# Two expert matrices loaded early, a modulation row read late, and the shared expert's down products moved six experts on

## What is computed

```python
sh_m, sc_m, g_m, sh_f, sc_f, g_f = modulations(c)          # each (9, 1024)
x = x + g_m * mixer(rmsnorm(x) * (1 + sc_m) + sh_m)
xn = rmsnorm(x) * (1 + sc_f) + sh_f
# 64 experts, 8 for each token, gates normalised and scaled by 2.5
hid = silu(xn @ exp_w_gate[e]) * (xn @ exp_w_up[e])          # 1024 -> 256
routed = sum over e of (hid * gate) @ exp_w_down[e]          # 256 -> 1024
shared = (silu(xn @ shared_w_gate) * (xn @ shared_w_up)) @ shared_w_down
y = rmsnorm(x + g_f * (routed + shared))
```

## Time and profile before

| | us |
|---|---|
| median of 3 runs | 806.15 |
| lowest, highest | 804.11, 809.91 |
| the profiled execution | 808.24 |
| its span, first to last instruction | 806.5 |
| TensorE busy in it | 704.0 |
| mean granted TensorE clock | 0.964 |

### The profile page before, as it was taken

One profiled execution on the slowest core, in us unless ns is written; L12 is line 12 of the kernel. 1 busy time (PEld: TensorE's weight loads), 2 busy tenths in 40 slices (PEclk: granted clock), 3 DMA queues, 4 the chain that ended last, 5 costly groups with the idle time before them and its releaser, 6 DMA issues.

```text
span 806.5 us, 14755 instructions
## 1 busy us (share of the span) xinstructions
PE 704.0 (87%) x4965; PEld 394.9 (49%) x4966; DVE 324.4 (40%) x601; ACT 228.2 (28%) x392; POOL 301.0 (37%) x317
## 2 busy tenths in 40 slices
PE   3699999999979999999999999998789978987820
PEld 1277556445554455554555555454355534544500
DVE  3115575477335553234332332434323434242217
ACT  4212622023123232223322322323222323232202
POOL 0321021021305454456544653636445454455220
PEclk9799999999989999999999999999999999999975
DMA  8999979729559999999999999999999999999943
GB/s 324 362 305 321 336 265 322 280 80 384 190 215 396 351 396 411 359 385 383 398 385 387 393 396 398 387 407 401 404 414 403 397 399 412 400 402 403 366 104 120
DMA packets 74813, 279.08 MB, mean 346 GB/s; under 512 B 18997, under 2 KB 22193, under 8 KB 49040
## 3 DMA queue, kind: packets, MB, share of 16 engines
q1 hardware_dynamic: 51240, 252.35, 78.9%
q0 software_dynamic: 23424, 26.07, 13.7%
q10 hardware_dynamic: 104, 0.08, 0.0%
HBM read 272.54 MB, written 26.30 MB: 371 GB/s over the span
## 4 chain that ended last, share of the span: by engine, by line
PE 64%; DMA 26%; DVE 4%; issue 2%; ACT 1%; SPq 1%; POOL 0%; POOLq 0%; DVEq 0%; ACTq 0%
PE bank L1118 27%; DMA gu<-in_exp_w_up 20%; PE bank L1154 11%; PE bank L863 5%; PE bank L854 5%; PE bank L981 3%; DMA gu<-in_ada_w 3%; PE bank L1096 2%; PE bank L829 2%; PE bank L1135 1%; PE bank L866 1%; PE bank L1210 1%; DMA sh<-in_shared_w_down 1%; PE bank L1065 1%; DMA sh<-acc_rows 1%
## 5 line engine op out<-in xcount | busy, mean ns | idle before, releaser
L1118 PE MATMUL bank<-gu,et 128*64 128x256 f32 x2496 | 286.7, 384 | 34.0 <-DMA gu<-in_exp_w_up 25.0
L1118 PEld LDWEIGHTS bank<-gu,et 128*64 128x64 f32 x2496 | 183.0, 138 | 155.5 <-issue 79.5
L537 POOL DMA_INDIRECT acc_rows<-et,idx x64 | 104.6, 1635 | 241.8 <-DVE et L1642 175.4
L1154 PE MATMUL bank<-dn,et 128*64 128x512 f32 x632 | 149.8, 603 | 11.9 <-issue 9.6
L1635 DVE COPY et<-bank 128x256 f32<-128x256 f32 x64 | 27.1, 424 | 259.8 <-PE bank L1135 259.8
L725 ACT ACTIVATE et<-bank 64x512 f32<-64x512 f32 x64 | 37.8, 591 | 266.9 <-PE bank L1118 266.9
L1154 PEld LDWEIGHTS bank<-dn,et 128*64 128x64 f32 x632 | 40.4, 136 | 78.8 <-issue 78.8
L735 ACT ACTIVATE et<-bank,mb 128x512 f32<-128x512 f32 x64 | 44.0, 687 | 119.8 <-PE bank L1154 104.2
L1642 DVE TENSOR_SCALAR et<-bank,mb 128x512 f32<-128x512 f32 x64 | 48.0, 751 | 68.3 <-PE bank L1154 58.5
L1628 DVE TENSOR_TENSOR et<-et 64x512 f32<-64x512 f32 x64 | 67.9, 1061 | 0.4 <-ACT et L726 0.4
L519 POOL DMA_INDIRECT et<-xn_rows,idx x32 | 35.7, 1116 | 55.4 <-DVE idx L1617 47.9
(11 more groups left out here) (290 smaller groups left out, 630.2 us busy)
## 6 DMA issues: line engine op xcount, KB each, us to landing
dn<-in_exp_w_down SPq DMA_DIRECT2D x64, 1024.0 KB, 25.0
gu<-in_exp_w_gate SPq DMA_DIRECT2D x63, 1024.0 KB, 22.7
gu<-in_exp_w_up SPq DMA_DIRECT2D x63, 1024.0 KB, 25.1
gu<-in_ada_w SPq DMA_DIRECT2D x12, 2048.0 KB, 14.6
gu<-in_w_in SPq DMA_DIRECT2D x3, 2048.0 KB, 19.3
gu<-in_w_out SPq DMA_DIRECT2D x2, 2048.0 KB, 16.7
acc_rows<-late SPq DMA_DIRECT2D x2, 1280.0 KB, 14.8
gu<-in_w_in SPq DMA_DIRECT2D x2, 1024.0 KB, 15.3
```

Of the source, the lines that this page charges most:

```text
L537: pool.indirect_dma_start(acc_rows[u % 2], bass.IndirectOffsetOnAxis(ap=idx[:, u, 0:1], axis=0), yo[:, u % 2, 0, :], None, bounds_check=2 ...
L1118: mm = pe.matmul(bank[u % 2][64 * c:64 * c + 64, b * FE:(b + 1) * FE], xt[:, b, k % 4, k // 4, :], w[c][:, k * FE:(k + 1) * FE], start=(k ...
L1154: mm = pe.matmul(bank[5 + b][64 * c:64 * c + 64, :], hT[:, b, j, :], dn[:, dslot(u), j * D + c * HALF:j * D + (c + 1) * HALF], start=(j == ...
```

## The change

1. SP loads expert 5's gate matrix into `gmod` once the residual is done with it (`x2_done`), and expert 4's up matrix into `late` once the counting matmuls are done (`counted`). Both stand ahead of `load_gu(0, 0, 3)`. Expert 5's up matrix stays in its place in `gu`.
2. GpSimd reads `g_f` into `gmod` not before the routing but in its group 0 at u == 7, behind gather(10) and scatter(6), after a wait for expert 5's matmuls.
3. ScalarE runs `moving_tokens(0, 2)` behind xt1(1) instead of ahead of it.
4. The six halves go with experts 8 to 13 instead of 2 to 7 (`SHARED_AT = 8`), on TensorE and on VectorE. TensorE's groups 2 and 3 and VectorE's group 1 are written out instead of looped.

```diff
+SHARED_AT = 8
+        gmodf = gmod[:, :, :].rearrange("p a n -> p (a n)")
...
-                sync.dma_start(guf[sl][:, 0:KT * FE], eg[e]).then_inc(ld_gu[sl], 16)
+                if not (isinstance(g, int) and g == SLOTS + 1):
+                    sync.dma_start(guf[sl][:, 0:KT * FE], eg[e]).then_inc(ld_gu[sl], 16)
                 sync.dma_start(guf[sl][:, KT * FE:2 * KT * FE], eu[e]).then_inc(ld_gu[sl], 16)
...
             for u in range(3):
                 load_dn(0, 0, u)
+            sync.wait_ge(s["acc_zeroed"], 32)
+            sync.wait_ge(ld_shared_gu, 32)
+            sync.wait_ge(s["x2_done"], 3)
+            sync.wait_ge(ld_gu[gslot(SLOTS + 1, SLOTS + 1)], 32)
+            sync.dma_start(gmodf, eg[SLOTS + 1]).then_inc(ld_gu[gslot(SLOTS + 1, SLOTS + 1)], 16)
+            sync.wait_ge(s["counted"], 1)
+            sync.dma_start(late[:, :], eu[SLOTS]).then_inc(ld_shared_gu, 16)
             load_gu(0, 0, 3)
-            sync.wait_ge(s["acc_zeroed"], 32)
             sync.dma_start(xTf[:, 0:KT * FE], eg[SLOTS]).then_inc(ld_shared_gu, 16)
-            sync.dma_start(late[:, :], eu[SLOTS]).then_inc(ld_shared_gu, 16)
...
             pool.wait_ge(s["gf_wrote"], 64)
-            get_mods(5, gmod[:, 0, :], gmod[0:64, 1, :], "gf_in")
...
                         scatter(r, i if u else i - 1, (u - 1) % U)
+                    if first and r == 0 and u == SLOTS + 3:
+                        pool.wait_ge(s["gu_done"], SLOTS + 2)
+                        get_mods(5, gmod[:, 0, :], gmod[0:64, 1, :], "gf_in")
...
                     gates(r, i, u)
-                    if first and r == 0 and u == 0:
-                        moving_tokens(0, 2)
                     if first and r == 0 and u == 1:
                         spread_table(0)
                     if not (last and u == U - 1):
                         xt1(r, i + (u + 1) // U, (u + 1) % U)
+                    if first and r == 0 and u == 0:
+                        moving_tokens(0, 2)
...
+                if isinstance(e, int) and e == SLOTS + 1:
+                    w = (gmodf, w[1])
...
-                    half = i * V + u - 2 if r == 0 and isinstance(i, int) and 2 <= i * V + u < U else None
+                    half = i * V + u - SHARED_AT if r == 0 and isinstance(i, int) and 0 <= i * V + u - SHARED_AT < 6 else None
...
-                    now_shared = first and r == 0 and u >= U - 6
-                    if now_shared and u % 2 == 0:
-                        shared_turned((u - U + 6) // 2)
+                    half = i * U + u - SHARED_AT if r == 0 and isinstance(i, int) and 0 <= i * U + u - SHARED_AT < 6 else None
+                    if half is not None and half % 2 == 0:
+                        shared_turned(half // 2)
...
-                    if now_shared:
-                        shared_sum(u - U + 6)
+                    if half is not None:
+                        shared_sum(half)
```

More of the change, by code:

```diff
@@ L1225, in rounds @@
                 body(r, 1)
-                with pe.Fori(2, NE // V - 1) as i:
+                body(r, 2)
+                body(r, 3)
+                with pe.Fori(4, NE // V - 1) as i:
                     body(r, i)
@@ L1688, in rounds @@
                 body(r, 0, first=True)
-                with dve.Fori(1, NE // U - 1) as i:
+                body(r, 1)
+                with dve.Fori(2, NE // U - 1) as i:
                     body(r, i)
```

## The result

The changed kernel takes 812.06 us (median of 12 runs, 808.25 to 816.71), the kernel before 806.19 beside it (804.11 to 809.91). The ratio is 1.0072, with a 95% interval of 1.0050 to 1.0094: 5.9 us slower. The forecast was 802.9 with a range of 796.5 to 809.0, so its sign was wrong, its case (within 1%) right, and the range ended 3 us too low. The profiled execution of after took 811.83 us, its span is 810.1.

What follows compares the result with a forecast made beforehand. Weights end the kernel, but TensorE before about 350 us, last at expert 13's end, decides how early they come. Terms 5.2 + 1.9 - 5.7 plus 1.8 of slack gave 3.2 us: 802.9 us against 806.15, range 796.5 to 809.

Steps and rivals of the forecast that it cites:

- The method: Find how much earlier TensorE reaches expert 13's end, add the weight queue's slack there, cap by the DMA engines.
- cap: DMA engines' limit on the gain: start 5.5 us earlier plus 6.0 us from 381 rising to 403 GB/s, 11.5 in all.
- step 5: Sum at expert 13's end: 5.2 + 1.9 - 5.7 = 1.4 us ahead, plus slack 1.8: 3.2 us; cap doesn't bind.
- sign: DMA share below 1 before 350 us, not released by expert 13, would mean the method itself is wrong.
- Step 1: ScalarE's new order at expert 1: TensorE starts 3.4 us earlier, runs at 2.4 GHz; 5.2 us ahead.
- Step 2: Halves moved from experts 2 to 7 to experts 8 to 13: 1.9 us ahead at expert 13's end, nothing at the end.
- Step 3: Two matrices loaded early, into DMA gaps before 240 us: shortens nothing, price 0; at most 5 us of loss.
- Step 4: Late modulation read behind scatter 6 lands at 297.3, due 291.6: TensorE stalls 5.7 us (3.6 to 7.5) before expert 8's down matmuls.
- Rival B: Modulation read lands much later; each us beyond 15.6 of latency delays the end; at 25 us, 9.4 us slower, 815.6; 8%.
- Rival A: Modulation read lands in time, within 6.7 us of issue, so nothing stalls: 8.9 us gained, 797.3; 16%.
- C: Start at expert 1 isn't won; early lead 0 to 3.3 us, sum 2.0 us slower to 1.3 faster: 806; 14%.
- D: Before 350 us small transfers, not TensorE, limit the rate; DMA stream starts 5.5 us earlier: 800.6 if stall covered; 12%.

Runs made afterwards that it cites:

- read_u5: The changed kernel with the late modulation read two experts earlier, behind scatter 4 instead of scatter 6: 807.43 us against 807.19 for the kernel before.
- halves_10: The changed kernel with the six halves behind experts 10 to 15 instead of 8 to 13, the read unmoved: 806.86 us against 807.19 for the kernel before.
- no_gmod: The changed kernel with expert 5's gate matrix in its ring place and the modulation read before the routing: 801.93 us against 807.19 for the kernel before.
- order_only: The kernel before with ScalarE's new order alone: 801.61 us against 807.19 for the kernel before.
- tiny_read: read_u5 with the late read cut to 16 bytes from one row, modulation not the reference's: 800.81 us against 805.76 for the kernel before.
- read_act: The changed kernel with the late reads issued by ScalarE, behind its copy of expert 7's tokens: 798.90 us against 805.76 for the kernel before.
- one_read: The changed kernel with the second read from one row instead of eight, modulation not the reference's: 811.26 us against 805.76 for the kernel before.
- halves_only: The kernel before with the six halves behind experts 8 to 13 and nothing else: 805.12 us against 806.76 for the kernel before.
- order_back: The changed kernel with ScalarE's old order: 817.75 us against 806.76 for the kernel before.
- early_up_40: halves_40 with expert 4's up matrix loaded early: 797.42 us against 806.03 for the kernel before.
- halves_40: The kernel before with ScalarE's new order and the six halves behind experts 40 to 45: 796.73 us against 806.03 for the kernel before.
- halves_40_old: The kernel before with the six halves behind experts 40 to 45 and ScalarE's old order: 802.44 us against 806.03 for the kernel before.
- halves_56_old: The kernel before with the six halves behind experts 56 to 61 and ScalarE's old order: 805.50 us against 806.76 for the kernel before.
- all_56: The changed kernel with the late reads issued by ScalarE and the halves behind experts 56 to 61: 803.05 us against 806.76 for the kernel before.
- halves_56: The kernel before with ScalarE's new order and the six halves behind experts 56 to 61, nothing else: 796.74 us, ratio 0.9872 to the kernel before.

## Why the prediction was wrong

**The method held.** In the ten changed kernels where the halves come before or around expert 13 (the rows after, read_u5, halves_10, no_gmod, order_only, tiny_read, read_act, one_read, halves_only and order_back), what TensorE has won or lost at the end of expert 13 arrives at the last expert within 1.4 us, from -6.2 to +10.5. For the six with more than 10 us of lead there, it doesn't: 15.5 us ahead becomes 7.6, and 10.3 becomes 2.1. A cap exists, as step 5 had it. The forecast had named a sign that would make the method itself wrong: a DMA share below 1 before 350 us that something other than expert 13 releases. By the letter it came, 0.52 from 325 to 330 us, ended by expert 11's matmuls. The sign was badly chosen: a late TensorE lets the queue run dry earlier too, and the last dry stretch, 350 to 355, still ends behind expert 13's matmuls, which end at 350.3.

**Step 1** was right: 5.2 us forecast, 5.0 in the trace, 5.2 in order_only's change at expert 13, and 5.2 in its time (ratio 0.9936).

**Step 2** forecast 1.9 us ahead at the end of expert 13; halves_only shows 0.3. There the six halves gave back 10.6 us up to expert 8's start (experts 2 to 8 in 39.5 us instead of 50.1), and five of them took 9.8 from there to expert 13's end (60.6 instead of 50.8): a half costs 1.77 us in the old place and 1.95 in the new, and 0.8 to 0.9 is left. Expert 1's slow matmuls then took 6.40 us instead of 5.82, both behind 4.5 us of idleness; the granted clock from 232.5 to 238.9 is 0.56 there and 0.66 in before, so the edit has no part in it. That leaves 0.3.

**Step 3**, price 0, was right: with the stall taken out (tiny_read) and alone (early_up_40) the early loads change nothing.

**Step 4 failed**: the stall was forecast as 5.7 us (3.6 to 7.5) and cost 12.5. Expert 9's start to expert 10's took 20.96 us, where an expert with a half takes some 8.5. It splits in two. The idle part was 9.6. The second read was issued at 281.1, 7.7 us before the data were due (I had 6.7), but landed in 17.2 us, not in 12.4. That is the step's wrong term. I took the mean of four earlier landings of the same instruction; all four were issued before the experts' gathers and scatters shared the queue, and the row nearest in kind, the 14.2 us, was already the largest. It had busy DMA engines beside it as well (share 1.02 and 1.03 from 189 to 199 us), and its like took 14.2 to 15.2 us in the eight other traces with an early read. So of the missing 4.8 us some 2 lie in the mean, and the rest appears only where the experts' own transfers share the queue; which of them is to blame was not tried. The idle part is 17.2 less 7.7, as step 4's own rule has it. Of the other 2.9 us, 2.6 are the clock: behind the idleness the down matmuls and the half ran at 1.2 GHz. I had counted exactly this as a gain of 2.1 us in step 1 and didn't apply it to the idleness that step 4 made.

**Step 5**: the slack of 0 to 3.4 us at expert 13, taken as 1.8, wasn't there. In the changed kernel the engines run dry at 350 to 355 as soon as TensorE is late. So the sum at the end of expert 13 is 5.0 + 0.9 - 12.5 = 6.6 us behind, by the halves' and the order's measured terms; the trace shows 6.1 behind, 6.0 arrive, and the medians differ by 5.9.

The cap was mis-sized too, though it didn't bind here. I let the rate rise from 381 to 403 GB/s. In halves_40 it rises to 392 with the queue fed, worth 109 us x (1 - 381/392) = 3.1 us, and 150 us x (1 - 392/394) = 0.8 behind that. With the 5.5 us of earlier start this makes 9.4 instead of 11.5; for halves_40_old and halves_56_old it makes 3.9, and for all_56, whose stretch of 241 to 350 runs at 389 GB/s and which moves 0.75 MiB of read into it (1.9 us at 403), 5.5 + 2.2 + 0.8 - 1.9 = 6.6. These sums use rates of the kernels that they explain, so they show consistency and forecast nothing. The traces agree within 1.4 us where expert 40 begins: TensorE is 10.4, 5.3, 5.0 and 6.9 us ahead there, in the same order. That a fed stream goes no faster than 389 to 395 GB/s before 500 us is measured in six kernels; why, against 401 to 403 behind, isn't settled. The share of time is 1.02 to 1.03 in both.

The rest of the shortfall is the halves themselves. Between the starts of experts 40 and 63 the lead falls by 2.8 to 3.2 us in each of the six kernels that have them there (10.4 to 7.6 in halves_40, 9.9 to 7.0 in halves_56), and moves by 0.6 at most in the ten others. So six halves cost some 3 us on TensorE even where weights end the kernel. By the medians halves_40 gains 9.3, which meets the 9.4 in part by luck.

**The rivals.** Rival B had the mechanism, the landing as the price and the end as the victim, but its break-even of 15.6 us of latency was too late: it contained the slack that didn't exist and lacked the slow clock. At 17.2 us it gives 1.6 us of loss, where 5.9 came. Rival A is out. C and D as well: the start was won, and the stream followed TensorE.

**What would have been better**, from the same runs: halves_40 or halves_56, at 796.7 us, 1.2 to 1.3% below before, with step 1 and the halves far behind and nothing of the rest.

## What to carry to other kernels

A transfer put late into a queue of small, latency-bound transfers is priced twice: by its own landing, with the queue's work in front of it and not by quiet landings of the same instruction, and by the landings of all that is issued behind it. If another engine's queue has room, issue it there: here that kept the gain (read_act), while an earlier place in the same queue (read_u5) or a later consumer (halves_10) didn't. Every stall added on TensorE costs its slow restart as well, and before a lead is counted, look at whether a fed queue really moves more than the thin one does.

## What the runs showed of the hardware

- A read of 256 KB behind one of 512 KB in GpSimd's queue landed in 16.2 to 17.5 us in five kernels (read_u5, halves_10, one_read, order_back, after), and the gathers issued behind such reads before they had landed took 17.0 to 19.2; with the reads in ScalarE's queue the gathers took at most 12.7.
- In the last part of the read the DMA engines were busy 1.00 to 1.03 of the time, but moved 342 and 327 GB/s in the two stretches of 5 us, against 409 in the stretch before, when the read was under way too, and 413 behind them. The weights' packets of 8 KB take longer there: 461 to 504 ns in the mean from 292 to 296, against some 310 before. one_read, with another form of the second read, moved 323 GB/s in 295 to 300, and read_act 333 from 276 to 282, so it isn't a matter of GpSimd's queue. Why it is only the last part is open.
- Behind 9.6 us of idleness TensorE ran at a granted clock of 0.50: 3.68 us for eight down matmuls that take 1.94, 2.85 for four matmuls of a half that take 1.99.
